# Two transformer blocks on one core: short extra products in TensorE's waits, three condition products moved ahead, and the recurrence's square sums split over two heads

## The chip, the core and the metric

The kernel runs on one core of a Trainium2 chip, in one launch. The metric is the device time of that launch in microseconds (us). The engines named here are TensorE (PE in the profile; its weight loads are PEld), VectorE (DVE), ScalarE (ACT), GpSimd (POOL) and SyncE (SP), which issues the large transfers. TensorE's clock has two levels, 1.2 and 2.4 GHz; the profile shows a granted clock of 0.50 and 1.00 for them.

## The reference

Everything is fp32, for 256 tokens of width 1024. The first block adds three things to x, each computed from a normalised x; the second block takes its result, and a condition vector c:

```
h = _rms(x, mix_norm_g[l])
p = h @ w_in[l]
a_out = _mla(...)                       # 8 heads, latent q and kv
h_out = _hyena(p[..., OFF_HY:], ...)    # long convolutions, here as DFT products
mixed = concatenate([_rms(a_out, ...), _rms(h_out, ...)])
x = x + mixed @ w_out[l]
x = x + _mem_xattn(_rms(x, ...), _rms(mem, ...), ...)   # 4 heads
x = x + _hier_moe(_rms(x, ...), ...)    # 4 groups x 8 experts, top 2 of a group, width 256

mod = silu(c) @ w_ada + b_ada           # six rows of 1024: sh1, sc1, g1, sh2, sc2, g2
u = modulate(x, sh1, sc1)
mix = hybrid_mixer(u, ...)              # gated recurrence (RG-LRU) beside attention of 8 heads
x = layernorm(DEEPNORM_ALPHA * x + g1 * mix, ln1_g, ln1_b)
ffn = hierarchical_moe(modulate(x, sh2, sc2), ...)
x = layernorm(DEEPNORM_ALPHA * x + g2 * ffn, ln2_g, ln2_b)
```

`mod` depends on c alone. The kernel computes it in twelve pieces of 512 columns, the *condition products* `ada(0)` to `ada(11)`, which may stand anywhere ahead of their use.

## The kernel before

**Order of work.** One stream of instructions is written by hand for each engine. TensorE goes, in this order: filter network, latent projection (`lat`), Hyena inputs and filter spectra (`hy0`, `hy1`, `hy2`), latent attention with `ada(0)` to `ada(5)` among its heads, the memory's transposes and projections (`memT`, `mk`, `mv`), output projection `wo`, `ada(6)`, `cT` and `mq`, four heads of cross attention (`xs`, `xT`, `xv`), their projection `mo`, the first mixture of experts, `ada(10)`, `ada(11)`, the inputs of the second block (`xl`, `aq`, `ga`, ...), eight heads of attention with the output projection's pieces (`wpa`, `wpb`) among them, and the second mixture of experts.

**Projections.** A weight arrives in a ring of four slots of SBUF (`ring`), loaded by SP's queue in the order of use. It is split into a high and a low part in fp32r: `high` (L471) on ScalarE, then `low` (L478) on VectorE, in four chunks of 128 x 1024, each holding two row blocks. `three_pass` (L613 to L615) then makes three products of each pair. Chunks 2 and 3 are split into the place of chunks 0 and 1, so ScalarE waits for those to have been used.

**PSUM.** The eight banks are given out by the list `STAGES`: each stage takes the next banks in turn, and `PLACE_AT` holds for each its bank and the number of earlier uses. `take` waits until the bank's earlier user has been read (`bank_free`), `full` and `got` hand it over, `free` gives it back. `transposed` (L598) makes 128x128 transposes by products with the identity `ident`.

**Condition products.** `ada(i)` (L736) is eight products of 32 x 512 in fp32, which the profile shows as 16 records. ScalarE copies the row into the weight's own ring slot (`ada_evac`, L1314), and `ada_col(i)` (L744) makes it a column by four products of one column each (8 records); `modulation(i)` on VectorE (L1851) reads that. The ring slot comes free after `ada_col`.

**A mixture of experts** (`moe(b)`, both times with the same code): transposes `rT` (L598), routing products `rt` (L894, 32 records of 36 columns), the choice of group and experts on VectorE (up to L2100, `hot`), the count of tokens ahead of each (`cnt`, L904 to L908), the selection matrices on VectorE (L2129, L2130, `sel`), the gathering products `gx` (L924), the transposed weights `swT` (L932), and then the loop over the experts: L949 (gate and up), L956, L963 (down) and L969. In the first mixture `ada_col(7)`, `ada(8)` and `ada_col(8)` stand between `rt` and `cnt`, and `ada(9)`, `ada_col(9)` and a bias product (L915) between `cnt` and `gx`.

**Attention of the second block.** Two heads' scores are made ahead (L1117, L1118); then for each head the probabilities are transposed (L1196), the next scores made, some other piece of work done and the values multiplied (L1208, L1209). In head 0 the other piece is `lss`: the sums of squares of the recurrence's output for both halves of the tokens (`token_sums`, L1166), 16 records of one column.

## Time and profile before

| | |
|---|---|
| runs (us) | 1061.04, 1061.32, 1060.31; median 1061.04 |
| profiled execution (us) | 1063.01 |
| its span, first to last instruction (us) | 1061.0 |
| mean granted TensorE clock | 0.955 |
| TensorE busy | 968.9 us (91%) |
| VectorE, ScalarE busy | 584.2 us (55%), 355.7 us (34%) |
| moved by DMA | 289.02 MB, mean 272 GB/s |

The profiled execution took 1.97 us more than the median of the timed runs, and 2.0 us of it lie outside its span. Busy shares are means over stages with different limits. A row of a timeline gives the start of an instruction (or of several alike), its length, its engine, line, kind and operands, and in brackets the idle time of the engine before it with what ended that. Lengths of products overlap, so the step between two starts is the better price of one. A row of windows gives, for a stretch, each engine's busy time, TensorE's granted clock (PEclk) and the DMA's share and rate.

### The profile page before, as it was taken

The numbers are of one execution on the slowest core, as the hardware profiler recorded it, in microseconds if no ns is written. First come the engines' busy times: TensorE is split into PE (matmuls) and PEld (weight loads), VectorE is DVE, ScalarE is ACT, GpSimd is POOL, SyncE is SP. The second block draws the span as 40 slices with busy tenths as digits, with TensorE's granted clock in tenths as the row PEclk, the third lists the DMA queues.
The fourth block names the chain that finished last, engine by engine and source line by source line (L and its number), as shares of the span: only waits on it lengthen the run. The fifth ranks groups of instructions, "written<-read, shape, count | busy, mean of one in ns | idle before, by whom it ended". The sixth has DMA issues, their size and how long they took to land.

```text
span 1061.0 us, 14615 instructions
## 1 busy us (share of the span) xinstructions
PE 968.9 (91%) x5146; PEld 582.0 (55%) x5146; DVE 584.2 (55%) x1104; ACT 355.7 (34%) x684; POOL 20.1 (2%) x41
## 2 busy tenths in 40 slices
PE   6999998999889799999999979898559999999985
PEld 5768556977766433343434569766443343434334
DVE  4735446556345546444444475766774755555545
ACT  5654325346334222222222365743521111111113
POOL 1000001000000000000000000000000000000000
PEclk9999999999997899999999989988769999999998
DMA  9253670455416699999999728530607999999941
GB/s 361 106 237 141 261 308 27 169 201 206 159 54 259 254 364 425 427 423 428 423 427 425 298 80 357 199 120 1 277 1 305 409 427 426 423 427 423 427 175 41
DMA packets 28894, 289.02 MB, mean 272 GB/s; under 512 B 3080, under 2 KB 5544, under 8 KB 7728
## 3 DMA queue, kind: packets, MB, share of 16 engines
q1 hardware_dynamic: 25344, 282.04, 64.9%
q0 software_dynamic: 1136, 3.74, 1.1%
q10 hardware_dynamic: 2368, 2.64, 0.8%
q8 instruction: 28, 0.46, 0.2%
q14 instruction: 18, 0.15, 0.0%
HBM read 287.34 MB, written 1.06 MB: 272 GB/s over the span
## 4 chain that ended last, share of the span: by engine, by line
PE 56%; DVE 6%; ACT 2%; issue 2%; DVEq 0%; ACTq 0%
PE bank L949 22%; PE bank L963 11%; PE bank L969 6%; PE bank L956 4%; PE bank L613 2%; PE bank L614 2%; PE bank L615 2%; PE bank L924 1%; PE bank L1069 1%; DVE ring_r L478 1%; PE bank L1070 1%; PE bank L1024 1%; PE bank L894 0%; PE bank L1208 0%; PE bank L1058 0%
## 5 line engine op out<-in xcount | busy, mean ns | idle before, releaser
L949 PE MATMUL bank<-ring,arena 128*64 128x512 f32 x1040 | 239.2, 602 | 6.6 <-DVE arena L2181 6.6
L478 DVE TENSOR_TENSOR ring_r<-ring,ring_r 128x1024 fp32r<-128x1024 f32 (+1 forms) x84 | 99.2, 1212 | 95.5 <-ACT ring_r L471 95.5
L2195 DVE TENSOR_REDUCE arena<-bank 128x512 f32 x130 | 83.8, 687 | 117.2 <-PE bank L969 114.6
L949 PEld LDWEIGHTS bank<-ring,arena 128*64 128x64 f32 x1040 | 69.8, 137 | 130.4 <-issue 130.4
L963 PE MATMUL bank<-ring,arena 128*64 128x512 f32 x520 | 125.8, 604 | 1.8 <-DVE arena L2317 1.4
L471 ACT ACTIVATE ring_r<-ring 128x1024 fp32r<-128x1024 f32 (+1 forms) x84 | 84.9, 1046 | 84.5 <-PE bank L615 84.0
L613 PE MATMUL bank<-HT_r,ring_r 128*128 128x256 f32 x352 | 103.9, 295 | 9.8 <-DVE arena_r L1795 3.6
L615 PE MATMUL bank<-HT_r,ring_r 128*128 128x256 f32 x352 | 101.9, 290 | 0.0
L1531 ACT ACTIVATE arena<-bank 128x512 f32<-128x512 f32 x64 | 38.3, 598 | 152.5 <-PE bank L949 152.5
L969 PEld LDWEIGHTS bank<-tab,arena 128*128 128x128 f32 x520 | 55.7, 140 | 54.8 <-issue 49.6
L613 PEld LDWEIGHTS bank<-HT_r,ring_r 128*128 128x128 f32 x352 | 70.3, 200 | 12.0 <-issue 10.5
L969 PE MATMUL bank<-tab,arena 128*128 128x128 f32 x520 | 70.9, 279 | 3.3 <-DVE arena L2224 2.1
L1525 ACT ACTIVATE arena<-arena 128x128 f32<-128x128 f32 x64 | 19.8, 309 | 152.7 <-DVE arena L2201 152.7
L615 PEld LDWEIGHTS bank<-HT_r,ring_r 128*128 128x128 f32 x352 | 70.0, 199 | 0.0
L614 PE MATMUL bank<-XN_r,ring_r 128*128 128x256 f32 x224 | 65.2, 291 | 0.0
L963 PEld LDWEIGHTS bank<-ring,arena 128*64 128x64 f32 x520 | 31.7, 136 | 50.8 <-issue 48.3
L956 PEld LDWEIGHTS bank<-tab,arena 128*128 128x128 f32 x260 | 27.2, 141 | 55.0 <-issue 50.3
L2201 DVE TENSOR_REDUCE arena<-bank 128x256 f32<-128x512 f32 x65 | 44.3, 681 | 14.3 <-PE bank L956 14.3
L615 PE MATMUL bank<-ring_r,arena_r 128*128 128x512 f32 x128 | 51.8, 404 | 0.0
L2181 DVE COPY arena<-arena 128x512 f32 x66 | 28.2, 427 | 36.5 <-issue 36.5
L614 PEld LDWEIGHTS bank<-XN_r,ring_r 128*128 128x128 f32 x224 | 45.0, 201 | 0.5 <-issue 0.5
L613 PE MATMUL bank<-ring_r,HT_r 128*128 128x512 f32 (+1 forms) x96 | 39.2, 408 | 5.9 <-DVE ring_r L478 5.1
(424 smaller groups left out, 1370.6 us busy)
## 6 DMA issues: line engine op xcount, KB each, us to landing
ring<-in_experts SPq DMA_DIRECT2D x64, 2048.0 KB, 15.1
ring<-in_experts SPq DMA_DIRECT2D x64, 1024.0 KB, 11.6
ring<-in_ada SPq DMA_DIRECT2D x12, 2048.0 KB, 8.7
ring<-in_win SPq DMA_DIRECT2D x5, 2048.0 KB, 12.8
ring<-in_hy SPq DMA_DIRECT2D x3, 2048.0 KB, 18.7
ring<-in_mk SPq DMA_DIRECT2D x2, 2048.0 KB, 8.5
ring<-in_mv SPq DMA_DIRECT2D x2, 2048.0 KB, 9.6
ring<-in_wo SPq DMA_DIRECT2D x2, 2048.0 KB, 7.4
```

Source lines behind the costliest of these rows:

```text
L471: nc.scalar.activation(R(h), w, ACT.Copy).then_inc(sem("w_high"), 1)
L478: nc.vector.tensor_tensor(R(w), w, R(h), ALU.subtract).then_inc(sem("w_low"), 1)
L613: mm(ps, R(ah), R(bh), start=first, stop=False)
L614: mm(ps, R(ah), R(bl), start=False, stop=False)
L615: return mm(ps, R(al), R(bh), start=False, stop=last_)
L949: last = mm(gu_bank[g:g + WIN, :], xw[:, k, :], w[:, k * 512:(k + 1) * 512], start=k < 2, stop=k >= KD - 2)
L956: last = tr(guT_bank[:, c * P:(c + 1) * P], gu_sb[:, c * P:(c + 1) * P], ident)
L963: last = mm(d_bank[half][64 * f:64 * f + WIN, :], hb[:, f, :], w[:, o:o + 512], start=True, stop=True)
L969: last = tr(dT_bank[c // 4][:, (c % 4) * P:(c % 4 + 1) * P], d_sb[:, c * P:(c + 1) * P], ident)
L1531: A_(gu_sb, gu_bank[:, :], ACT.Copy).then_inc(sem(f"gu_sb{b}"), 1)
L2195: last = V.reduce_sum(ysT[:, 4 * u:4 * u + 4, bass.ds(s, WIN)], dT_bank[u][:, :].rearrange("p (c g w) -> p c w g", c=4, g=2), AXX)
L2201: return V.reduce_sum(three(gu_sum, 4), guT_bank[:, :].rearrange("p (c g w) -> p c w g", c=4, g=2), AXX)
```

## The change

A helper `occupy(stage, j, n)` is added on TensorE. It waits for the bank that stage `stage` will take next, and issues `n` fp32 products of 128x128 by 128x256 into it (16 records for eight of them); the stage's own first product starts anew and overwrites them. It is called in twenty places, for 106 products in all: ahead of the filter network (8), `lat` (5), `hy2` (4), `mk` (5), `cT` (3), `xs0` (2), `xT0` (3), `mo` (1), the first `gx` (6) and the first expert loop (8), `ada(10)` (4), `xl` (4), `aT0` (4), in heads 3 and 4 (4 and 4), `rT2` (21), `cnt2` (8), the second `gx` (8), and the second expert loop (4). The operands are tables that are in SBUF anyway; the first two calls read an area of zeros, `still`, that VectorE sets at its start.

`ada(7)` moves ahead of `mo`, `ada(8)` takes the place of `ada(7)`, `ada_col(7)` goes ahead of the routing products, and `ada_col(8)`, `ada(9)`, `ada_col(9)` all stand between `rt` and `cnt`. ScalarE's copies follow: `ada_evac(7)` before the second half of `mo`'s first weight is split, `ada_evac(8)` where 7 was and `ada_evac(9)` where 8 was. VectorE's `modulation(9)` goes from behind the selection to directly behind the count. The order of SP's loads is unchanged. The list `STAGES` follows, so from `mo` on the stages lie in banks shifted by one.

The sums of squares `lss` are made in two halves, one in head 0 and one in head 1; VectorE's copy of them goes from head 0 to head 1.

```diff
-STAGES += [("mo", 4), ("ada7", 1)]
+STAGES += [("ada7", 1), ("mo", 4), ("ada8", 1)]
...
+            def occupy(stage, j, n, w=ident, x=T("iota")[:, 0:256]):
+
+                b, use = place(stage, j)
+                if use:
+                    pe.wait_ge(sem(f"bank_free{b}"), use)
+                for _ in range(n):
+                    mm(bank[b][:, 0:256], w, x, start=True, stop=True)
...
+            pe.wait_ge(sem("still"), 1)
+            occupy("hT", 0, 8, still[:, 0:P], still[:, P:P + 256])
...
             transposed("hT", XN, KD, "xn_x")
+            occupy("lat", 0, 5, still[:, 0:P], still[:, P:P + 256])
...
+            occupy("hy2", 0, 4)
             channel_out("hy2", ["hy2"], HT, low_x, banks_of("hT"))
...
             transposed("memT", XN, KD, "xn_m")
+            occupy("mk", 0, 5)
...
             ada(6)
+            occupy("cT", 0, 3)
...
+            occupy("xs0", 0, 2)
...
+            occupy("xT0", 0, 3)
...
+            ada(7)
+            occupy("mo", 0, 1)
             token_out("mo", ["mo0", "mo1"], oT, low_m, [(f"xv{h}", 0) for h in range(XH)])
-            ada(7)
+            ada(8)
 
             def moe(b):
+                if b == 2:
+                    occupy("rT2", 0, 21)
                 transposed(f"rT{b}", XN, KD, f"xn_r{b}")
+                if b == 1:
+                    ada_col(7)
...
                 if b == 1:
-                    ada_col(7)
-                    ada(8)
                     ada_col(8)
+                    ada(9)
+                    ada_col(9)
+                else:
+                    occupy("cnt2", 0, 8)
 
                 pe.wait_ge(sem("hot"), b)
...
                 if b == 1:
-                    ada(9)
-                    ada_col(9)
                     pe.wait_ge(sem("onehot"), 32)
...
+                occupy(f"gx{b}", 0, 8 if b == 2 else 6)
...
+                occupy(f"yTa{b}", 0, 8 if b == 1 else 4)
...
+            occupy("xl", 0, 4)
             ada(10)
             ada(11)
             transposed("uT", XN, KD, "xn_u")
+            occupy("xl", 0, 4)
             channel_out("xl", ["win0"], HT, low_x, banks_of("uT"))
...
                     a_scores(1)
+                    occupy("aT0", 0, 4)
...
                 if h == 0:
                     pe.wait_ge(sem("squared"), 4)
-                    full(token_sums(take(pe, "lss"), sq, range(4)), "lss")
+                    lss = take(pe, "lss")
+                    token_sums(lss, sq, range(4), (0,))
+                    wp_ps["lss"] = lss
                 elif h == 1:
+                    full(token_sums(wp_ps["lss"], sq, range(4), (1,)), "lss")
                     pe.wait_ge(sem("lo_low"), 1)
                     wp_lru(0, 0)
                 elif h == 2:
                     wp_lru(0, 1)
+                elif h == 3:
+                    occupy("ap2", 0, 4)
                 elif h in (4, 5):
+                    if h == 4:
+                        occupy("ap2", 0, 4)
                     wp_lru(1, h - 4)
...
             x_out(XH - 1)
+            ada_evac(7)
             high(act, "mo0", (2, 3))
...
-            ada_evac(7)
+            ada_evac(8)
...
                 if b == 1:
-                    ada_evac(8)
+                    ada_evac(9)
                 act.wait_ge(sem("e_diff"), b)
...
+            V.memset(still, 0.0).then_inc(sem("still"), 1)
...
                                      ALU.add), f"cnt{b}")
+                if b == 1:
+                    modulation(9)
...
                 if b == 1:
-                    modulation(9)
                     ready(dve, "adac9")
...
-                if h == 0:
+                if h == 1:
                     ps = got(dve, "lss")
```

Three places on TensorE. The first is the first mixture of experts from the routing products' end (`wr,HT`, 36 columns) to the gathering products (`arena_r`, 512 columns); 32 x 512 is a condition product, 128 x 1 its column, 128 x 32 the count. Before:

```order
L894 MATMUL bank<-wr,HT 128x36
L744 MATMUL bank<-tab,ring 128x1 [waits bank_free6,bank_free0]
L744 MATMUL bank<-tab,ring 128x1 x3
L736 MATMUL bank<-ring,cm 32x512 [waits bank_free7,slot_full0]
L736 MATMUL bank<-ring,cm 32x512 x7
L744 MATMUL bank<-tab,ring 128x1 [waits bank_free0,bank_free7]
L744 MATMUL bank<-tab,ring 128x1 x3
L904 MATMUL bank<-arena,tab 128x32 [waits bank_free1,hot]
...
L736 MATMUL bank<-ring,cm 32x512 [waits bank_free2,slot_full1]
L736 MATMUL bank<-ring,cm 32x512 x7
L744 MATMUL bank<-tab,ring 128x1 [waits bank_free3,bank_free2]
...
L915 MATMUL bank<-HT 8x512 [waits bank_free4,mask_row,onehot]
L924 MATMUL bank<-arena_r 128x512 [waits bank_free5,xn_low,sel1]
```

The same place after the change, where `bank<-tab 128x256` are the added products:

```order
L756 MATMUL bank<-tab,ring 128x1 [waits bank_free0,bank_free1]
L756 MATMUL bank<-tab,ring 128x1 x3
L748 MATMUL bank<-ring,cm 32x512 [waits bank_free1,slot_full1]
L748 MATMUL bank<-ring,cm 32x512 x7
L756 MATMUL bank<-tab,ring 128x1 [waits bank_free2,bank_free1]
L756 MATMUL bank<-tab,ring 128x1 x3
L930 MATMUL bank<-arena,tab 128x32 [waits bank_free3,hot]
...
L939 MATMUL bank<-HT 8x512 [waits bank_free4,mask_row,onehot]
L600 MATMUL bank<-tab 128x256 [waits bank_free5]
L600 MATMUL bank<-tab 128x256 x5
L950 MATMUL bank<-arena_r 128x512 [waits bank_free5,xn_low,sel1]
```

Between `rt` and `cnt` one column, one condition product and one column stand as before, each of the next number; between `cnt` and `gx` a condition product and its column are gone and six added products stand in their place.

The second place is the second mixture of experts after the change, from the last projection to the gathering products. Before, the rows are the same without those of `bank<-tab 128x256`:

```order
L625 MATMUL bank<-ring_r,arena_r 128x512
L600 MATMUL bank<-tab 128x256 [waits bank_free7]
L600 MATMUL bank<-tab 128x256 x20
L608 MATMUL bank<-tab,XN 128x128 [waits bank_free2,bank_free1,normed,bank_free0,bank_free7]
...
L918 MATMUL bank<-wr,HT 128x36
L600 MATMUL bank<-tab 128x256 [waits bank_free4]
L600 MATMUL bank<-tab 128x256 x7
L930 MATMUL bank<-arena,tab 128x32 [waits bank_free4,hot]
...
L600 MATMUL bank<-tab 128x256 [waits bank_free5]
L600 MATMUL bank<-tab 128x256 x7
L950 MATMUL bank<-arena_r 128x512 [waits bank_free5,xn_low,sel2]
```

Each group of added products stands directly ahead of an instruction that waits for another engine.

The third place is heads 0 and 1 of the second block's attention, where 128x1 are the sums of squares. Before, all of them stand in head 0:

```order
L1118 MATMUL bank<-arena 128x256
L1166 MATMUL bank<-tab,arena 128x1 [waits bank_free5,squared]
L1166 MATMUL bank<-tab,arena 128x1 x7
L1208 MATMUL bank<-arena 64x256 [waits bank_free5,bank_free3,bank_free4,bank_free2]
L1209 MATMUL bank<-arena 64x128
L1196 MATMUL bank<-tab,arena 128x128 [waits bank_free2,a_norm]
```

After the change:

```order
L1197 MATMUL bank<-tab,arena 128x1 [waits bank_free5,squared]
L1197 MATMUL bank<-tab,arena 128x1 x3
L1246 MATMUL bank<-arena 64x256 [waits bank_free5,bank_free3,bank_free4,bank_free2]
L1247 MATMUL bank<-arena 64x128
L1234 MATMUL bank<-tab,arena 128x128 [waits bank_free2,a_norm]
L1234 MATMUL bank<-tab,arena 128x128 x2
L1147 MATMUL bank<-arena 128x128 [waits bank_free1]
L1148 MATMUL bank<-arena 128x256
L1197 MATMUL bank<-tab,arena 128x1 x4
L623 MATMUL bank<-ring_r,arena_r 128x512 [waits bank_free7,w_low,bank_free6,lo_low]
```

Half of the one-column products has gone behind head 0's values and head 1's transposes and scores.

## Rows read from the trace of the kernel before

**Rows 1.** The page's part 1: busy time, share of span, instructions.

```profile
PE 968.9 (91%) x5146; PEld 582.0 (55%) x5146; DVE 584.2 (55%) x1104; ACT 355.7 (34%) x684; POOL 20.1 (2%) x41
```

**Rows 2.** Windows: start:end length, busy PE, PEld, DVE, ACT, POOL, PEclk, DMA share, GB/s.

```profile
75.00:85.00 10.00, 7.84 (x55) 7.63 (x54) 6.35 (x11) 7.23 (x13) 0.00 (x0) 0.83 0.84 357
...
296.00:304.00 8.00, 5.00 (x16) 3.83 (x15) 3.56 (x4) 2.38 (x4) 0.00 (x0) 0.79 0.00 0
324.00:370.00 46.00, 39.20 (x188) 24.97 (x188) 25.53 (x74) 13.73 (x32) 1.16 (x3) 0.74 0.70 281
370.00:600.00 230.00, 228.69 (x1164) 92.31 (x1160) 111.47 (x213) 52.26 (x102) 0.00 (x0) 1.00 0.99 416
...
686.00:750.00 64.00, 56.32 (x238) 40.63 (x234) 41.09 (x90) 23.94 (x61) 0.90 (x2) 0.84 0.18 72
750.00:800.00 50.00, 25.60 (x118) 19.73 (x118) 36.34 (x84) 20.50 (x44) 1.12 (x2) 0.73 0.36 145
800.00:1016.00 216.00, 215.64 (x1099) 86.08 (x1100) 122.23 (x231) 29.70 (x64) 0.00 (x0) 1.00 1.00 417
```

**Rows 3.** Waits of PE: line and releaser, us in total, times, longest.

```profile
PE bank L613 <- DVE ring_r L478: 11.2, 5, 3.0
```

**Rows 4.** Timeline of PE, fp32 products of 128x256 at full clock.

```profile
277.51 3.69 PE L864 MATMUL bank<-arena 128*128 128x256 f32 x16 [1.10 <-issue]
```

**Rows 5.** Timeline of PE, the latent projection's first products.

```profile
15.17 0.68 PE L613 MATMUL bank<-ring_r,HT_r 128*128 128x416 f32 x1 [2.77 <-DVE ring_r L478]
...
21.16 0.35 PE L613 MATMUL bank<-ring_r,HT_r 128*128 128x416 f32 x1
21.34 0.35 PE L614 MATMUL bank<-ring_r,HT_r 128*128 128x416 f32 x1
```

**Rows 6.** A window over those products.

```profile
15.00:20.00 5.00, 4.83 (x14) 4.65 (x15) 2.52 (x6) 3.13 (x6) 0.00 (x0) 1.00 0.98 420
```

**Rows 7.** Timeline of PE, the first product of `mo`.

```profile
300.57 0.76 PE L613 MATMUL bank<-ring_r,arena_r 128*128 128x512 f32 x1 [3.00 <-DVE ring_r L478]
```

**Rows 8.** Timeline of PE, first mixture of experts.

```profile
329.45 5.33 PE L894 MATMUL bank<-wr,HT 128*128 128x36 f32 x32 [1.05 <-ACT HT L1259]
...
342.45 0.61 PE L904 MATMUL bank<-arena,tab 128*128 128x32 f32 x2
...
344.70 3.64 PE L736 MATMUL bank<-ring,cm 128*32 128x512 f32 x16
...
351.00 9.18 PE L924 MATMUL bank<-arena_r 128*128 128x512 f32 x32
...
365.33 5.35 PE L949 MATMUL bank<-ring,arena 128*64 128x512 f32 x16 [4.28 <-DVE arena L2181]
```

**Rows 9.** Timeline of DVE, there: second half of the selection.

```profile
348.58 0.75 DVE L2130 SCALAR_TENSOR_TENSOR arena_r<-tab,arena,arena_r 128x512 fp32r<-128x512 f32 x1
```

**Rows 10.** Timeline of PE, the second block's first projection.

```profile
622.16 0.55 PE L613 MATMUL bank<-HT_r,ring_r 128*128 128x256 f32 x1 [2.43 <-DVE XN_r L2382]
```

**Rows 11.** Timeline of PE, attention of the second block.

```profile
688.82 0.47 PE L613 MATMUL bank<-ring_r,HT_r 128*128 128x512 f32 x1 [2.31 <-DVE ring_r L478]
...
697.22 1.95 PE L1166 MATMUL bank<-tab,arena 128*128 128x1 f32 x16
...
716.96 1.11 PE L1208 MATMUL bank<-arena 128*64 128x256 f32 x2 [2.39 <-DVE arena L2509]
...
723.45 0.77 PE L613 MATMUL bank<-ring_r,arena_r 128*128 128x512 f32 x1 [2.54 <-issue]
```

**Rows 12.** Timeline of PE, second mixture of experts.

```profile
761.88 3.35 PE L598 MATMUL bank<-tab,XN 128*128 128x128 f32 x16 [12.31 <-DVE XN L2567]
...
775.03 0.64 PE L904 MATMUL bank<-arena,tab 128*128 128x32 f32 x2 [4.95 <-DVE arena L2100]
...
782.00 9.09 PE L924 MATMUL bank<-arena_r 128*128 128x512 f32 x32 [4.62 <-DVE arena_r L2130]
...
796.01 3.65 PE L949 MATMUL bank<-ring,arena 128*64 128x512 f32 x16 [2.33 <-DVE arena L2181]
```

More of the change, by code:

```diff
@@ L188 @@
     STAGES += [(f"xT{_h}", 1)] + ([(f"xs{_h + 2}", 1)] if _h + 2 < XH else []) + [(f"xv{_h}", 1)]
-STAGES += [("mo", 4), ("ada7", 1)]
+STAGES += [("ada7", 1), ("mo", 4), ("ada8", 1)]
 def _moe_stages(b):
-    ada = [[(f"ada{i}", 1), (f"adac{i}", 1)] if b == 1 else [] for i in (8, 9)]
-    return [(f"rT{b}", 4), (f"rt{b}", 1)] + [("adac7", 1)] * (b == 1) + ada[0] + [(f"cnt{b}", 1)] + ada[1] + [("bias", 1)] * (b == 1) + [(f"gx{b}", 8), (f"swT{b}", 2)] \
+    one = b == 1
+    return [(f"rT{b}", 4)] + [("adac7", 1)] * one + [(f"rt{b}", 1)] + [("adac8", 1), ("ada9", 1), ("adac9", 1)] * one \
+        + [(f"cnt{b}", 1)] + [("bias", 1)] * one + [(f"gx{b}", 8), (f"swT{b}", 2)] \
         + [("g2r", 2)] * (b == 2) + [(f"yTa{b}", 4), (f"sct{b}", 4), (f"yTb{b}", 4)]
@@ L336, in two_blocks @@
         prod = three(area(13312, 1024), TT)
+        still = area(12288, 384)
         krb = three(area(13312, 256), TT)
@@ L936, in moe @@
                     gate_row("g2r", diag2, "diag2")
+                occupy(f"yTa{b}", 0, 8 if b == 1 else 4)
+                if b == 2:
                     for j in range(2):
@@ L1160, in wp_attention, with token_sums @@
                     full(last, *stage)
-            def token_sums(ps, src, chunks):
-                for t in range(TT):
+            def token_sums(ps, src, chunks, ts=range(TT)):
+                for t in ts:
                     for i in chunks:
@@ L1498, in moe @@
                 if b == 1:
-                    ada_evac(9)
                     ps = got(act, "bias")
```

## The prediction

> **What bounds the kernel now.** I read the busy times first: TensorE works 91% of the span, the others 55% or less [rows 1], so TensorE's stream sets the time, and only two things can shorten it: fewer or shorter waits, and products that run at the higher clock. The table of windows comes next [rows 2]. In both expert loops TensorE is busy for 228.69 of 230 us and 215.64 of 216 at granted clock 1.00. These 446 us can't gain; they move with their start. The clock is below 1.00 elsewhere. It has two levels, so a mean of 0.84 over 64 us means 64 x (1 - 0.84) / 0.5 = 20.5 us at 1.2 GHz. In the same way the six shorter windows hold: 3.4 us (75:85), 3.4 (296:304), 23.9 (324:370), 20.5 (686:750), 27.0 (750:800); 170:180 and 600:630 look like the first (0.83, 0.89). Whoever works through such a stretch at 2.4 GHz saves half of its busy part. Third come the timelines around them. Nearly all of these stretches begin with a wait of TensorE of 2.2 to 12.3 us for VectorE or ScalarE: 2.77 [rows 5], 3.00 [rows 7], 4.28 [rows 8], 2.43 [rows 10], 2.31, 2.39 and 2.54 [rows 11], 12.31, 4.95 and 4.62 [rows 12]. Five waits for the split of a weight alone are 11.2 us [rows 3]. The exception is the loop's second start: 2.33 us idle, and yet its first 16 records take 3.65 us, where those of the first loop took 5.35 after 4.28 [rows 8, 12]. So an idle time above some 2 us costs the clock in most cases, not in all.
>
> **Price of a product added.** Sixteen records of 128x256 in fp32, which are eight products, take 3.69 us at the higher clock [rows 4]: 0.44 us a product with the tail of the last, and so 0.88 at 1.2 GHz. Where a wait is longer than its products the cost is nothing, since TensorE would stand still. VectorE's memset at the start is cover too: TensorE waits for a DMA there.
>
> **Part by part, as gains in us.**
> Start. `lat` begins cold after 2.77 us: 14 records in 4.83 us are 0.345 each, against 0.18 later [rows 5, 6]. Fifteen such steps at the higher clock would give 2.4. Five products in front take 2.2 us warm and 4.4 cold, 1.6 more than the wait, so the bounds are +2.4 and -1.6; I take 0.5, because the products in front are themselves the cold ones.
> The Trainium skill, "TensorE: Matmul & The Clock Gate", Part 1, warns that the clock recorded in trn2 traces can be unreliable. The row of the window agrees: it shows 1.00 where the steps are twice as long. By the record alone this term would be nothing, by the steps it is up to 2.4.
> `hy2` and `mk`. Each has some 3.4 us at 1.2 GHz (75:85, and 170:180 like it [rows 2]) behind a wait; the one of `hy2` is among the five for a split weight, 2.2 us in the mean and 3.0 the longest [rows 3]. Half of 3.4 is 1.7, the bound. The other bound is the overrun, 4 x 0.88 - 2.2 = 1.3 and 5 x 0.88 - 3.0 = 1.4 lost. The waits are short against what a cold start takes, so not all is saved: 1.3 and 1.2.
> `cT`, `xs0`, `xT0`: two or three products in front of waits of 1 to 2 us, no cold stretch behind: 0 (+0.3 to -0.8 together).
> `mo`. The moved `ada(7)`, 16 records of 32x512, lies now in the wait of 3.00 [rows 7] with one product more: at half of the cold price of the same form (3.64, [rows 8]) 1.9 + 0.4 = 2.3, it fits. ScalarE's copy of it falls where ScalarE has nothing to do until chunk 0 is used. Window 296:304 gives 1.7 at most, and chunk 2's split follows chunk 0's end, so the gain passes on: 1.6; worst -1.0 (4.0 cold against 3.0).
> First routing. Between `rt` and `cnt` the same number of columns and condition products stands as before, so with the clock as it is `cnt` starts as before. What changes is behind it. The selection was done at 348.58 + 0.75 = 349.33, but TensorE came to `gx` only at 351.00, since `ada(9)` began at 344.70 [rows 8, 9]: 1.7 us late. With `ada(9)` gone, the six products and the bias fill 4.6 us; cold at first, they are done near 349.7. That gives 1.3. `gx` took 9.18 with half of it cold, about 7.3 if warm: 1.9 more, if the six products raise the clock. Against it VectorE's `modulation(9)` now stands in front of the selection (0.2). If the clock even holds through `rt`, the way from 329.45 to `cnt` (13.0) loses up to 4 more; VectorE's choice then is the limit. Bounds 0 and 7.0. The 36-column products let the clock fall in both mixtures, so I take near the low end: 2.5.
> First expert. Eight products, 3.5 us warm, fit in 4.28; 5.35 becomes 3.65 [rows 8, 12]: 1.7. The loop's loads start when the columns of the condition products are made, which is earlier as well, so the loop doesn't run into them, though its DMA share is 0.99.
> `xl`. Behind 2.43 us [rows 10] the cold stretch is 6.6 us (600:630 at 0.89), but its second half waits for a weight chunk that ScalarE splits after other work. Bounds +1.5 and -1.0: 0.
> Attention. The 20.5 cold us of window 686:750 are three stretches, by the steps of the single products: 3.4 behind 688.82, 6.6 from 700, the rest from 717. Products in front of 688.82 save 1.5; the sixteen one-column records at 697.22 stand right ahead of the second stretch (half is 3.3), and halving them may or may not keep the clock; the weight's split follows the scores by 5.6 us and takes back 0.8 of it. The products in front of 716.96 change nothing by themselves, as 723.45 waits for VectorE's chain; those in front of that save 1.7 [rows 11]. Bounds 3.2 - 1.3 of overruns = 1.9, and 5.7: 4.0.
> Second routing. 21 products last 9.2 us, of 12.31 idle. 3.1 us stay idle, so the transposes (3.35) probably start cold as before: 0, at best 1.3. Eight products in 4.95: half cold, as `rt` ends cold, 4 x 0.88 + 4 x 0.44 = 5.3, 0.3 over; `cnt` warm saves 1.1. Eight in 4.62, warm, fit; `gx` from 9.09 to some 7.3: 1.8. Sum 2.6, less a part for a clock that may not rise in time: 2.2; bounds -2.1 (eight cold products, 7.0) and 3.9. Four products in 2.33 fit, and the loop was warm already: 0.
> The skill's same page, Part 4, says of TensorE's transpose mode that it doesn't count as busy for the clock. The row shows them once only, at 3.35 us behind a long idle time [rows 12], which fits both. If the 16 transposes behind the 21 products were idle in that sense, the products would have been for nothing and `rt` would start cold: the second routing would then give 1.3 instead of 2.2.
>
> Sum: 0.5 + 1.3 + 1.2 + 1.6 + 2.5 + 1.7 + 4.0 + 2.2 = 15.0. The profiled 1063.01 becomes 1048.0; it lies 1.97 over the median, so the timed runs go from 1061.04 to 1046.0.
>
> **The rivals.**
> *Half is given back.* The clock still falls behind short waits, and ScalarE's and VectorE's chains take over in attention and routing, whose ends don't depend on TensorE's clock. For it: L478 releases five waits, and 716.96 and 723.45 are of that kind. Against: the first expert and both `gx` need only the clock. Half of 15: 1053.5.
> *All waits keep the clock.* Upper bounds but for the start: 1.0 + 1.6 + 1.6 + 1.7 + 6.0 + 1.7 + 1.0 + 5.5 + 3.5 = 23.6, 1037.4. For it: almost every cold stretch stands behind a wait that is now filled. Against: the narrow products of 36, 32 and 1 columns remain.
> *Slower: the added products run at 1.2 GHz.* They stand behind narrow or short work, at 0.88 each. Overruns: `lat` 1.6, `hy2` 1.3, `mk` 1.4, `mo` 1.0, first `gx` 1.7, first expert 7.0 - 4.3 = 2.7, `xl` 1.1, `aT0` 1.2, heads 1.1 and 1.0, `cnt2` 2.1, second `gx` 2.4, second loop 1.2, together 19.8. In place of that, what follows would be warm at half of these places at least, since the products went before it, about 8: 1061 + 12 = 1073. It decides from a step of over 0.6 us a product at most places. Against: 0.23 to 0.44 in every wide fp32 stretch that follows warm work, as most waits do.
> *Nothing happens.* The clock follows something other than the waits, and the waits swallow all products: 1061. Only the later `gx` against `ada(9)` speaks for a gain even then, 1.3, so this is nearly excluded.
>
> **How the numbers follow.** Forecast 0.55; half given back 0.22; all waits warm 0.15; slower 0.06; nothing 0.02. Range 1038 to 1055. It holds the forecast, most of the half and the greater part of the full gain. A measurement of this kernel can tell about 0.2%, 2.1 us, from no change: faster by more 0.92, within it 0.03, slower 0.05.
>
> **What would show it.** Right: a granted clock of 1.00 in the stretches behind `hy2`, `mk` and `mo`; 0.44 us a product in the groups of `mo`, the first expert and the second `gx`; the first 16 records of the first loop in 3.65; `gx` starting within 0.5 us of the selection, and both in under 8 us; 324:370 shortened by over 4. Wrong: products of 0.88 that end after their wait; the clock at 0.50 in 717:727 or behind 689 as before; a loop that waits for its weights. If the gain is under 8, the terms of attention and of first routing are those to doubt.

## The result, and the profile after

The changed kernel took 1053.12 us (median of 11 runs, 1048.18 to 1058.38), the kernel before 1061.67 us beside it (11 runs). The ratio is 0.990, 95% interval 0.9872 to 0.9929: 7.5 to 13.6 us faster, where 15.0 were forecast, 1046.0 with a range of 1038 to 1055. The medians are 8.6 us apart, the two profiled spans 9.8. (The text on the change says that the added products stand in twenty places; its list has nineteen.)

TensorE's row of busy times after the change (before: [rows 1]). Its busy time grows by 35.0 us. The 212 added records alone take 56.3 us, so the rest of its work got 21 us shorter.

```profile
PE 1003.9 (96%) x5358; PEld 611.3 (58%) x5358; DVE 584.0 (56%) x1105; ACT 355.2 (34%) x684; POOL 20.2 (2%) x41
```

The same windows as in [rows 2], in the same columns (start:end length, busy PE, PEld, DVE, ACT, POOL, granted clock, DMA share, GB/s):

```profile
75.00:85.00 10.00, 9.57 (x72) 8.94 (x71) 7.54 (x12) 7.21 (x13) 0.00 (x0) 1.00 0.70 295
...
296.00:304.00 8.00, 7.48 (x33) 5.99 (x33) 3.40 (x4) 2.86 (x4) 0.00 (x0) 1.00 0.00 1
324.00:370.00 46.00, 43.77 (x194) 29.39 (x196) 23.63 (x71) 11.52 (x25) 1.17 (x3) 0.78 0.71 293
370.00:600.00 230.00, 228.36 (x1167) 95.72 (x1164) 113.91 (x216) 52.50 (x102) 0.00 (x0) 1.00 0.98 411
...
686.00:750.00 64.00, 60.45 (x265) 44.97 (x264) 40.26 (x84) 24.12 (x60) 0.90 (x2) 0.89 0.24 92
750.00:800.00 50.00, 44.16 (x215) 29.98 (x213) 33.65 (x84) 17.19 (x36) 1.12 (x2) 0.93 0.40 153
800.00:1016.00 216.00, 214.31 (x1094) 86.38 (x1092) 124.55 (x234) 27.23 (x60) 0.00 (x0) 1.00 0.97 409
```

The windows around `hy2` and `mo` went from 0.83 and 0.79 to 1.00. The stretch of the first routing hardly moved, 0.74 to 0.78, and attention little, 0.84 to 0.89. Those two are where the forecast was too high.

The sharpest view is the start of the instruction at the same place in both traces. Each difference is the sum of all gains before it:

| instruction | before | after | difference |
|---|---|---|---|
| filter network's second layer, behind the first part of `lat` | 22.38 | 20.99 | -1.39 |
| `mk`, first product | 174.90 | 172.19 | -2.71 |
| `mo`, first product | 300.57 | 296.66 | -3.91 |
| condition product behind `mo` (`ada(7)` before, `ada(8)` after) | 324.33 | 318.83 | -5.50 |
| first `gx` | 351.00 | 346.09 | -4.91 |
| first `swT` | 360.01 | 353.58 | -6.43 |
| `ada(10)`, behind the first mixture | 613.08 | 604.95 | -8.13 |
| columns of `ada(10)`, behind `xl` | 636.41 | 629.11 | -7.30 |
| first `av` product | 688.82 | 681.49 | -7.33 |
| square sums, head 0 | 697.22 | 689.09 | -8.13 |
| `wp0`, first product, head 1 | 702.30 | 695.05 | -7.25 |
| last projection's piece behind head 4 | 723.45 | 716.81 | -6.64 |
| transposes of the second mixture | 761.88 | 755.00 | -6.88 |
| second `gx` | 782.00 | 773.36 | -8.64 |
| second loop, first product | 796.01 | 785.84 | -10.17 |
| span | 1061.0 | 1051.2 | -9.8 |

TensorE's timeline after the change, at the places of [rows 7, 8]:

```profile
296.66 0.47 PE L623 MATMUL bank<-ring_r,arena_r 128*128 128x512 f32 x1 [0.52 <-DVE ring_r L480]
...
323.95 5.64 PE L918 MATMUL bank<-wr,HT 128*128 128x36 f32 x32 [0.26 <-ACT HT L1297]
...
337.26 0.61 PE L930 MATMUL bank<-arena,tab 128*128 128x32 f32 x2
...
341.31 5.13 PE L600 MATMUL bank<-tab 128*128 128x256 f32 x12
346.09 7.65 PE L950 MATMUL bank<-arena_r 128*128 128x512 f32 x32
...
358.90 3.65 PE L977 MATMUL bank<-ring,arena 128*64 128x512 f32 x16 [0.83 <-DVE arena L2221]
```

`mo` waits 0.52 us instead of 3.00, and its first product takes 0.47 instead of 0.76. The first expert's records take 3.65 instead of 5.35. The six products ahead of `gx` took 5.13 us, 0.80 each by the step from their start to that of `gx`: the granted clock is 0.50 from 341.3 to 345.3 and rises in the last of them (0.68 in 345.3 to 346.3). VectorE was done long before they ended:

```profile
334.26 0.23 DVE L2139 TENSOR_TENSOR arena<-arena 128x64 f32<-128x64 f32 x1
...
343.39 0.75 DVE L2171 SCALAR_TENSOR_TENSOR arena_r<-tab,arena,arena_r 128x512 fp32r<-128x512 f32 x1
```

The choice (`hot`) was there at 334.5 and the count started at 337.26, 2.8 us late; the selection was there at 344.1 and `gx` started at 346.09, 2.0 late.

`xl`, where the second chunk ends, the third begins, and the clock falls [rows 10]:

```profile
619.74 0.28 PE L625 MATMUL bank<-HT_r,ring_r 128*128 128x256 f32 x1
621.79 0.36 PE L623 MATMUL bank<-HT_r,ring_r 128*128 128x256 f32 x1 [1.77 <-DVE ring_r L480]
...
622.48 0.41 PE L625 MATMUL bank<-HT_r,ring_r 128*128 128x256 f32 x1
```

Attention [rows 11]:

```profile
679.11 1.99 PE L600 MATMUL bank<-tab 128*128 128x256 f32 x8
681.49 0.47 PE L623 MATMUL bank<-ring_r,HT_r 128*128 128x512 f32 x1 [0.39 <-DVE ring_r L480]
...
689.09 1.02 PE L1197 MATMUL bank<-tab,arena 128*128 128x1 f32 x8 [0.73 <-ACT arena L1345]
...
690.92 0.90 PE L1234 MATMUL bank<-tab,arena 128*128 128x128 f32 x3
...
693.33 1.86 PE L1197 MATMUL bank<-tab,arena 128*128 128x1 f32 x8
695.05 0.77 PE L623 MATMUL bank<-ring_r,arena_r 128*128 128x512 f32 x1
...
700.45 0.86 PE L1246 MATMUL bank<-arena 128*64 128x256 f32 x2
...
716.81 0.47 PE L623 MATMUL bank<-ring_r,arena_r 128*128 128x512 f32 x1 [2.37 <-issue]
717.12 0.40 PE L624 MATMUL bank<-ring_r,arena_r 128*128 128x512 f32 x1
...
718.07 0.63 PE L625 MATMUL bank<-ring_r,arena_r 128*128 128x512 f32 x1
```

The stretch behind 681.49 is warm now, but 0.73 us of that are waited off at once: TensorE comes to the square sums before ScalarE's squares are ready, a wait that did not exist. By 690.92 the clock is down (0.90 against 0.55 for these three transposes at full clock), so the second half of the square sums costs 1.86 us where one half costs 1.02 warm. Behind 716.81 the clock falls after five products.

The eleven runs of the changed kernel say the same in another way. Their spans go from 1046.2 us at a granted clock of 0.981 to 1056.2 at 0.968; a straight line through all eleven has 0.80 us per 0.001 of clock and a correlation of -0.99. What differs from run to run is mainly how long the clock is low. A single trace, and the table above, are one draw of that. At most places they are good for some 1 us; at the first routing and in `xl` for less, as the traces of the experiments show at their end.

### The profile page after: what moved, and what is told of

Same layout as the page of the kernel before. It is cut to its first block, busy times and chain, and to the rows that moved or that the text cites. A ratio compares the mean times of both kernels' runs of the same rounds, so it can differ in the third digit from the quotient of the medians.

```text
span 1051.2 us, 15040 instructions
## 1 busy us (share of the span) xinstructions
PE 1003.9 (96%) x5358; PEld 611.3 (58%) x5358; DVE 584.0 (56%) x1105; ACT 355.2 (34%) x684; POOL 20.2 (2%) x41
## 4 chain that ended last, share of the span: by engine, by line
PE 54%; DVE 7%; ACT 2%; issue 2%; DVEq 0%; ACTq 0%
PE bank L977 22%; PE bank L991 11%; PE bank L997 6%; PE bank L984 4%; PE bank L623 2%; PE bank L625 2%; PE bank L624 2%; DVE ring_r L480 1%; PE bank L950 1%; PE bank L1097 1%; PE bank L1098 1%; PE bank L1052 1%; PE bank L1246 0%; PE bank L1197 0%; PE bank L918 0%
## 5 line engine op out<-in xcount | busy, mean ns | idle before, releaser
L623 PE MATMUL bank<-HT_r,ring_r 128*128 128x256 f32 x352 | 101.9, 290 | 6.0 <-DVE ring_r L480 3.1
L625 PE MATMUL bank<-HT_r,ring_r 128*128 128x256 f32 x352 | 100.3, 285 | 0.0
L997 PE MATMUL bank<-tab,arena 128*128 128x128 f32 x520 | 70.9, 279 | 3.3 <-DVE arena L2264 2.1
L623 PEld LDWEIGHTS bank<-HT_r,ring_r 128*128 128x128 f32 x352 | 68.2, 194 | 8.9 <-issue 7.3
L625 PEld LDWEIGHTS bank<-HT_r,ring_r 128*128 128x128 f32 x352 | 68.2, 194 | 0.0
L600 PE MATMUL bank<-tab 128*128 128x256 f32 x186 | 47.7, 409 | 0.0
L984 PE MATMUL bank<-tab,arena 128*128 128x128 f32 x260 | 42.6, 286 | 2.1 <-ACT arena L1569 1.4
```

The costliest lines, as they stand in the source:

```text
L600: mm(bank[b][:, 0:256], w, x, start=True, stop=True)
L623: mm(ps, R(ah), R(bh), start=first, stop=False)
L625: return mm(ps, R(al), R(bh), start=False, stop=last_)
L984: last = tr(guT_bank[:, c * P:(c + 1) * P], gu_sb[:, c * P:(c + 1) * P], ident)
L997: last = tr(dT_bank[c // 4][:, (c % 4) * P:(c % 4 + 1) * P], d_sb[:, c * P:(c + 1) * P], ident)
```

## The experiments

Theory A is the prediction's: the added products keep the clock for what follows. Rival B: the moved condition products carry the gain. All experiments are compared with the kernel before on the same chip.

**e1_moves_only.** Moves and split stay, the products go.

```diff
             def occupy(stage, j, n, w=ident, x=T("iota")[:, 0:256]):
-                b, use = place(stage, j)
...
+                return
```

> The changed kernel without any of the 106 added products; the moved condition products and the split square sums stay. Theory A (the gain is TensorE's clock behind filled waits): only ada(7) in the wait ahead of mo (up to 1.6 us) and the routing without ada(9) ahead of gx (up to 1.5) are left, so about 1058 to 1061 against 1061.0 before, and the first expert's 16 records are at 5.3 us again. Rival B (the moved condition products carry the gain): 1053 to 1055.

Measured: 1061.26 us against 1061.39, ratio 0.9997 (0.9975 to 1.0018). The moved parts together are worth nothing that can be measured. That is a sum of two: from `mo`'s first product to the condition product behind it this trace takes 22.17 us, as the changed kernel does, where the kernel before took 23.76, so `ada(7)` alone fills that wait and is worth 1.6 us; the split of the square sums takes about as much back (e3_lss_whole). The first expert is cold again behind its old wait:

```profile
360.09 5.35 PE L973 MATMUL bank<-ring,arena 128*64 128x512 f32 x16 [4.29 <-DVE arena L2217]
```

**e2_fill_only.** The kernel before with the products alone.

```diff
+            occupy("mo", 0, 5)
             token_out("mo", ["mo0", "mo1"], oT, low_m, [(f"xv{h}", 0) for h in range(XH)])
...
+                if b == 2:
+                    occupy("gx2", 0, 8)
```

> The kernel before with the added products alone, at the same places and in the same numbers, but 5 ahead of mo (ada(7) isn't there to fill that wait) and none ahead of the first gx, where TensorE comes late anyway. Theory A: start 1.4, hy2 and mk 2.5, mo 1.6, first expert 1.7, second routing 2.4, attention and xl near 0: about 9.5 off, 1051.5 (1050 to 1054). Rival B: under 3 off, 1058 or more.

Measured: 1051.04, ratio 0.9921 (0.9892 to 0.9951). The whole gain, or as much as can be told, comes with the products. Rival B falls; what the moved `ada(7)` wins at `mo`, five products win there as well (22.19 us).

**e3_lss_whole.** The square sums in head 0 again.

```diff
-                    lss = take(pe, "lss")
-                    token_sums(lss, sq, range(4), (0,))
-                    wp_ps["lss"] = lss
+                    full(token_sums(take(pe, "lss"), sq, range(4)), "lss")
```

> The changed kernel with the sixteen one-column square sums all in head 0 again. Theory C (splitting them doesn't hold the clock, as it fell in head 0 all the same, and the second half then costs 1.86 us at 1.2 GHz): the same as the changed kernel or up to 1 us faster. Rival D (the split is worth something, my term of the prediction): slower by 1.5 to 3 us.

Measured: 1051.61, ratio 0.9909 (0.9883 to 0.9935), against 0.990 for the changed kernel. The times can't decide, since the 1.5 to 3 us of rival D lie within the interval. The traces can. From the first square sum to the values of head 1 it takes 10.02 us here:

```profile
688.02 1.92 PE L1197 MATMUL bank<-tab,arena 128*128 128x1 f32 x16 [0.72 <-ACT arena L1342]
...
698.04 0.65 PE L1243 MATMUL bank<-arena 128*64 128x256 f32 x2
```

With the split it takes 11.36 us (689.09 to 700.45). The other traces agree: whole sums 10.01 to 10.08 (before, e2, e3, e6, e7, e8), split ones 11.36 to 11.64 (after, e1, e5, e10, e11). The exception is e9, where the clock held through both halves (6.93). The 1.5 us are still there at the second mixture's transposes, 64.34 us behind the first sum here and 65.91 in the changed kernel. Rival D falls: the split is a loss of some 1.5 us, more than theory C had.

**e4_narrow.** Two products of one column for each of 256.

```diff
-                for _ in range(n):
-                    mm(bank[b][:, 0:256], w, x, start=True, stop=True)
+                for _ in range(2 * n):
+                    mm(bank[b][:, 0:1], w, x[:, 0:1], start=True, stop=True)
```

> The changed kernel with each added product of 256 columns replaced by two of one column each, which take TensorE about as long (8 records of one column took 0.95 us before, so 0.48 for two products against 0.44). Theory E (the clock looks at how much is computed, not at whether TensorE is idle): the waits are filled but the clock falls as before, so most of the gain of the filling is lost: 1058 to 1061, first expert 5.3 us. Rival F (any instruction in the wait keeps the clock): 1053 as the changed kernel.

Measured: 1071.30, ratio 1.0098 (1.0066 to 1.0131), worse than either expected. The expectation took their warm price. At 1.2 GHz two such products last 0.9 us, and the 42 ahead of the transposes last longer than the wait of 12.3 there: 15.8 us, and not 19 as the next expectation says.

```profile
747.40 15.84 PE L600 MATMUL bank<-tab 128*128 128x1 f32 x84
763.10 3.65 PE L608 MATMUL bank<-tab,XN 128*128 128x128 f32 x16
```

No time is idle ahead of these transposes, and they are as slow as behind 12.31 us of idle time. The cleanest place is the first expert:

```profile
356.61 3.63 PE L600 MATMUL bank<-tab 128*128 128x1 f32 x32
361.06 5.07 PE L977 MATMUL bank<-ring,arena 128*64 128x512 f32 x16 [0.82 <-DVE arena L2221]
```

The narrow products last as long as the wide ones (3.63 against 3.62) and leave as much idle (0.82 against 0.83), at a granted clock of 1.00 until 360, and yet the expert's records take 5.07 against 3.65. So theory E holds in the traces; the time mixes it with the overruns, so it was run again with one for one.

**e10_narrow_once.** The same, `range(n)`.

> The changed kernel with each added product narrowed from 256 columns to one, one for one; such a product takes 0.24 us warm and 0.46 cold, so nothing overruns its wait, unlike in e4_narrow, where two for one at 1.2 GHz took 19 us in a wait of 12. Theory E (the clock falls although TensorE isn't idle): as e1_moves_only, 1059 to 1062. Rival F (filling the wait with anything is enough): 1053 to 1055.

Measured: 1062.96, ratio 1.0008 (0.9985 to 1.0031): nothing is left of the gain. TensorE's timeline, first mixture:

```profile
344.56 2.72 PE L600 MATMUL bank<-tab 128*128 128x1 f32 x12
347.44 10.13 PE L950 MATMUL bank<-arena_r 128*128 128x512 f32 x32 [0.17 <-DVE arena_r L2171]
...
358.29 1.84 PE L600 MATMUL bank<-tab 128*128 128x1 f32 x16
...
362.74 5.35 PE L977 MATMUL bank<-ring,arena 128*64 128x512 f32 x16 [2.61 <-DVE arena L2221]
```

`gx` takes 10.13 against 7.65 behind products of 256 columns. The clock was already at 0.50 when the six began, in both kernels; the wide ones brought it up just ahead of `gx`, the narrow ones did not, and `gx` is as slow as in e1 with nothing there (10.35). At other places the shorter products leave much idle, 2.61 us ahead of the first expert and 7.73 ahead of the second mixture's transposes, so there this run can't tell narrow work from idle time; e4's traces can. The time fits theory E: nothing is left of the gain when the products have one column.

**e5_routing.** Work that isn't awaited leaves the way to the count.

```diff
                     ada_col(8)
-                    ada(9)
-                    ada_col(9)
...
+                    ada(9)
+                    ada_col(8)
...
                 if b == 1:
+                    ada_col(9)
                     pe.wait_ge(sem("onehot"), 32)
...
-                occupy(f"gx{b}", 0, 8 if b == 2 else 6)
+                occupy(f"gx{b}", 0, 8 if b == 2 else 1)
```

> The changed kernel with the first routing in another order: between rt and the count stand ada(9) and then ada_col(8) (5.5 us cold, for a choice on VectorE of 4.9), behind the count ada_col(9), the bias product and 1 added product instead of 6; modulation(9) back behind the selection. Theory G (in the changed kernel TensorE comes 2.9 us late to the count and 2.0 late to gx, for work that could stand elsewhere): the count starts within 0.6 us of the choice, gx within 0.5 of the selection, some 4 us earlier; gx itself stays at 1.2 GHz longer, +1.5; net 2 to 3 us faster than the changed kernel, 1050. Rival H (gx's start doesn't matter, the clock takes it all back): as the changed kernel, 1053.

Measured: 1047.42, ratio 0.9868 (0.984 to 0.9896). TensorE's timeline:

```profile
328.16 3.46 PE L748 MATMUL bank<-ring,cm 128*32 128x512 f32 x16
331.55 1.05 PE L756 MATMUL bank<-tab,ring 128*128 128x1 f32 x8
333.19 0.41 PE L929 MATMUL bank<-arena,tab 128*128 128x32 f32 x2 [0.58 <-DVE arena L2139]
...
339.34 8.61 PE L950 MATMUL bank<-arena_r 128*128 128x512 f32 x32 [0.34 <-DVE arena_r L2169]
```

From the routing products' end to `gx` it is now 11.2 us (328.16 to 339.34), where the changed kernel took 16.7 (329.40 to 346.09); `gx` itself gives 1.0 back. TensorE now waits for VectorE at both places, as it should. Theory G holds in the trace. The gain over the changed kernel is 3.4 us by the ratios, whose intervals overlap.

**e6_att_rT2_empty.** e2 without the products in attention (heads 3 and 4 too, not shown) and without the 21.

```diff
-                    occupy("aT0", 0, 4)
...
-                if b == 2:
-                    occupy("rT2", 0, 21)
```

> The kernel before with the added products alone (as in e2_fill_only), but without those in attention (ahead of aT0, in heads 3 and 4) and without the 21 ahead of rT2. Theory I (attention is bounded by VectorE's and ScalarE's chain and by the cold stretch behind the one-column products, which the fillers don't reach; rT2's products end 3 us before the transposes): no slower than e2_fill_only by more than 1 to 1.5 us, 1052. Rival J (my term of 4 us for attention holds and other noise hid it): 1055 or more.

Measured: 1054.12, ratio 0.9932 (0.9911 to 0.9952) against 0.9921 for e2: 1.2 us, inside the interval. In time these 33 products can't be told from nothing. The traces say more. From the first square sum to the second mixture's transposes e2 takes 64.38 us and e6 65.71; the kernel before, without them as well, took 64.66. So the products of heads 3 and 4 win between 0.3 and 1.3. At the second `gx` the two are level again (768.74 and 768.81), since in e2 the eight products ahead of the count ran at 1.2 GHz (6.37 us) and ended 1.1 us after VectorE's choice (761.82, the count at 762.92). The transposes with the 21 products, and without:

```profile
736.37 9.23 PE L599 MATMUL bank<-tab 128*128 128x256 f32 x42
748.84 3.42 PE L607 MATMUL bank<-tab,XN 128*128 128x128 f32 x16 [3.24 <-DVE XN L2601]
```

```profile
750.10 3.65 PE L607 MATMUL bank<-tab,XN 128*128 128x128 f32 x16 [12.31 <-DVE XN L2594]
753.73 3.96 PE L912 MATMUL bank<-wr,HT 128*128 128x36 f32 x32
```

With 3.24 us left idle the transposes are nearly as slow as behind 12.31.

**e7_more_fill.** e2 with the remaining waits filled (also 10 products instead of 8 ahead of the second `gx`, not shown).

```diff
+            channel_out("xl", ["win0"], HT, low_x, banks_of("uT"),
+                        between=lambda c: occupy("adac10", 0, 4) if c == 1 else None)
...
-                        occupy("ap2", 0, 4)
+                        occupy("ap2", 0, 8)
...
-                    occupy("rT2", 0, 21)
+                    occupy("rT2", 0, 28)
```

> As e2_fill_only with more added products: 4 between the second and third chunk of xl (a wait of 1.8 us that is new, in which the clock falls), 8 instead of 4 in head 4 (2.4 us left), 28 instead of 21 ahead of rT2 (3.2 us left), 10 instead of 8 ahead of the second gx (1.3 left). By theory A each keeps the clock for what follows: xl 1.7, head 4 1.6, transposes and rt 1.5 to 2, gx 0.2: 5 us off e2_fill_only, 1046 to 1047. Rival K (these stretches are bounded by the chains of ScalarE and VectorE, a warm TensorE only waits longer): 1051.

Measured: 1048.83, ratio 0.9876 (0.9849 to 0.9902), 4.8 us under e2 by the ratios, 2.2 by the medians, the intervals overlapping. The transposes:

```profile
736.32 12.25 PE L599 MATMUL bank<-tab 128*128 128x256 f32 x56
748.79 1.94 PE L607 MATMUL bank<-tab,XN 128*128 128x128 f32 x16 [0.22 <-DVE XN L2603]
751.33 5.29 PE L915 MATMUL bank<-wr,HT 128*128 128x36 f32 x32 [0.61 <-ACT HT L1296]
```

They are warm, 1.94 for 3.42, but 0.61 is waited off and the 36-column products lose the clock in their midst (5.29 for 4.44): of 1.5 us, 1.2 remain at the count. In head 4, with eight products and 0.64 us idle, the twelve products of the weight take 2.93 us instead of 4.51 and the 1.5 us gained reach the transposes (62.83 us behind the first square sum, 64.38 in e2). At `xl` nothing was won: from its first product to the columns of conditions it takes 13.54 us here and 13.57 in e2, where the clock had held behind 1.75 us of idle time. Theory A holds where the stretch was cold, and the sizes are smaller than thought.

**e11_gx1_none.** The changed kernel without the six products ahead of the first `gx` (`8 if b == 2 else 0`).

> The changed kernel without the six products ahead of the first gx, which ran at 1.2 GHz there (5.1 us) and ended 2 us after the selection. Theory L (an added product that delays real work costs its whole time, the same work cold costs half): gx starts 2 us earlier and has 2 to 3 us more at 1.2 GHz: 0.5 to 1 us faster than the changed kernel, 1052.5. Rival M (they warm gx and pay for themselves): 1 us slower, 1054.

Measured: 1050.95, ratio 0.9894 (0.9858 to 0.993), the changed kernel's 0.990.

```profile
343.14 10.09 PE L950 MATMUL bank<-arena_r 128*128 128x512 f32 x32 [2.86 <-issue]
```

`gx` starts 2.95 us earlier and takes 2.44 longer. This trace was ahead by 0.95 us at the condition product behind `mo` (317.88 against 318.83) and is ahead by 0.51 at `swT` (353.07 against 353.58), so here the six products are worth 0.4 us, less than one pair of traces can tell. Neither theory L's gain nor M's loss is shown; the six products about pay for themselves.

**e9_double.** Twice as many products everywhere (`range(2 * n)`).

> The changed kernel with twice as many added products everywhere. What my slower rival rested on, measured by itself: products beyond a wait cost TensorE 0.44 us each if the clock is up, 0.88 if not. 106 more are 46.6 us at 0.44; about 14 us of idle time are left at these places to take them, and stretches that were still cold (xl, head 4, the transposes of rT2) become warm, about 4: 1053 + 47 - 14 - 4 = 1082 (1078 to 1086) if the clock stays up. 1110 or more if the products themselves run at 1.2 GHz.

Measured: 1065.69, ratio 1.0026 (0.9995 to 1.0057), 16 us less than expected. The price per product was right: the added records take 101.4 us of TensorE against 56.3, so 0.43 us for each of the 106 more. What was wrong is that an overrun travels on to the end. Against the changed kernel the trace is 10.8 us late at the first expert and 9.8 at the square sums, but only 4.4 at the values of head 5 (725.57 against 721.19). Of these 5.4 us, 4.4 are won up to the values of head 1, where the clock held, and the rest in waits for VectorE and ScalarE that got shorter. By the second expert loop it is 13.7 us late, for the products ahead of the second mixture's transposes, count and `gx` overrun their waits too. In all, 45 us of added work cost 13.6 us of span. The prediction's rival that had the change slower at 1073 summed its overruns in the same way, so it was probably priced too high as well.

**e8_all.** The changed kernel with the square sums whole, e5's order and e7's additions.

> The changed kernel with the square sums whole, e5's routing and e7's additions: if both hold, 1053 - 2.5 - 5 = 1045 to 1046; if neither, 1052.

Measured: 1046.03, ratio 0.9847 (0.9818 to 0.9876), the lowest: 16 us under the kernel before, 5.6 us under the changed one by the ratios. Its interval overlaps those of e5 and e7. Its profiled span is 1042.8 us at a granted clock of 0.984.

**What the traces say together.** Each line is a stretch of TensorE's stream, from the start of one instruction to the start of another, by trace:

| stretch | us |
|---|---|
| first mixture, `rt` to `swT`, order of the kernel before | before 30.56, e7 27.83, e2 27.74, e6 26.14 |
| the same, order of the changed kernel | after 29.63, e3 29.62; without wide products e11 30.06, e10 30.04, e1 28.45 |
| the same, order of e5 | e5 25.01, e8 24.96 |
| `xl`, first product to the columns of conditions | before 14.25; after and e11 15.08, e3 15.06; e1, e2, e5 13.57, e6, e8 13.56, e7 13.54, e10 13.53 |
| first square sum to the second mixture's transposes, sums whole | before 64.66, e6 65.71, e2 64.38, e3 64.34, e7 62.83, e8 62.82 |
| the same, sums split | after 65.91, e11 66.00, e5 66.02, e10 66.37, e1 66.42 |
| first expert, its first 16 records | 3.65 in the eight with wide products ahead; before, e1, e10 5.35; e4 5.07 |

The same instructions in the first routing took from 26.14 to 30.56 us, and the trace of the kernel before is the longest of the four. `xl` took 13.5 or 15.1 us in the changed kernel's variants, with products in its waits or without. So a single pair of traces settles neither place.

## Why the prediction was right, and where it was not

Direction and mechanism were right: the gain comes with the added products (e1, e2), and it goes when they have one column (e4, e10). The size was about two thirds, and the measured time lies near the upper end of the range. Of the terms, with what the table of starts shows for each:

Start, 0.5 taken: 1.4. `lat` began 0.9 us later but warm. Here the steps between products, 0.19 us instead of 0.345, told the truth, and not the record of the clock, which is 1.00 in both.

`hy2` and `mk`, 1.3 and 1.2: 1.3 and 1.2. `mo`, 1.6: 1.6. First expert, 1.7: 1.7. The reading was: a window's mean clock gives the cold time, half of its busy part is the gain, if the wait in front takes the products. It held wherever the work behind the wait was wide and TensorE alone bounded it.

First routing, 2.5: 0.9. The step that failed is "cold at first, they are done near 349.7": the six products ran at 1.2 GHz to nearly their end, behind work that had been at 1.2 GHz since the routing products, and `gx` came 2.0 us after the selection. I had seen that the 36-column products let the clock fall, and didn't carry it on to the six. Also not seen: the columns of conditions behind `rt` made the count 2.8 us late, before and after; e5 took those. Even the 0.9 is against the slowest of four traces of the old order; against the other three (26.1 to 27.8 us) the changed order, at 29.6, is slower.

`xl`, 0: -0.8. In this trace the clock fell in a new wait of 1.77. In e2 it held behind 1.75, so this loss is a draw of the single trace.

Attention, 4.0: -0.45. This is the mis-sized term, the largest of the sum and 4.4 of the 5 us missing. The saving of 1.5 behind 688.82 was there, and half of it was waited off at ScalarE's squares (0.73). "Halving them may or may not keep the clock": it did not. The clock fell 1.6 us behind the first square sum (690.7, at 0.84 in 690 to 691), 2.7 us behind it before, the second half was then made at half speed, and the split lost 1.5 us (e3). And "those in front of that save 1.7": four products left 2.37 us idle and the clock fell five products on; with eight instead of four, e7 gained 1.5 of these 1.7. As they stand, the products in heads 3 and 4 are worth 0.3 to 1.3 us by the traces (e6), and nothing that the times can tell.

Second routing, 2.2: 3.3, for the most part by `cnt` and `gx` warm, as reasoned: 0.9 from the count to `gx` and 1.5 from `gx` to the loop. The rest is 0.5 at the transposes and 0.3 up to the count; whether that comes of the 21 products isn't shown.

Of the signs that were named, these came: a clock of 1.00 behind `hy2`, `mk` and `mo`, some 0.45 us a product ahead of the first expert and of the second `gx`, the first loop's 3.65, both `gx` under 8 us. These did not: the first `gx` started 2.0 us after the selection, and from the condition product behind `mo` to the first expert it is 40.07 us instead of 41.00, nothing near 4 less.

Of the rivals, "half is given back" at 1053.5 came nearest in time; by the ratio, 10.6 us, the gain lies about midway between it and the forecast. Its reason is there in part: 0.73 us are waited off at ScalarE's squares. What it lacks is that clock was lost behind narrow work too, in the first routing and in head 0. That its figure comes so near is in part luck, since the loss at `xl` is a draw. The slower case did not come, because its products were warm at most places. In the kernel before, TensorE did nothing from 749.6 to 761.88 and then nothing but the 16 transposes until 765.2, and the granted clock rose among them (0.50 until 764, 0.61 in 764 to 765, 1.00 behind); in e7 they ran warm throughout behind 28 products. So these traces don't bear out for these transposes what the Trainium skill, "TensorE: Matmul & The Clock Gate", Part 4, says of the transpose mode, that it doesn't count as busy for the clock.

## What to carry to other kernels

Where an engine's clock depends on its work, look for waits ahead of wide work and fill them to the end with wide throwaway products; here a group that left 3 us idle was worth almost nothing, and one with one column nothing. Fill only waits that are there: first move work that nobody awaits out of the way of what VectorE awaits (3.4 us here by the ratios), then fill what remains. Count a gain only up to the next instruction that waits for another engine's chain, and check that the work behind isn't narrow. Before one place is judged by one pair of traces, compare the same stretch in several.

## What the runs showed of the hardware

Work of one column in TensorE's waits lost the higher clock as if little had run: behind 32 records of one column and 0.82 us of idle time the first expert took 5.07 us, behind 16 of 256 columns, as long in time, and 0.83 us of idle time 3.65 (e4). The clock fell in the midst of the 36-column products of the first mixture too, with 0.26 us of idle time ahead of them (granted clock 1.00 in 324 to 325, 0.73 in 325 to 326, 0.50 behind). Narrow work doesn't always cost it: in e9, with no idle time ahead, twice eight records of one column took 1.05 us each and the clock stayed at 1.00.

Idle times of 1.31 us (second `gx`) and 1.75 (`xl` in e2) kept the clock, 1.77 (`xl` in the changed kernel) and 2.37 (head 4) lost it a few products on, and 2.33 ahead of the second loop kept it in the kernel before.

The granted clock varies between runs of one program, 0.968 to 0.981 here, and 0.80 us of span go with each 0.001. With such a spread, five rounds settle some 3 us, and not the single places; those only the traces tell, and several of them.

That the first `gx` costs about the same with six cold throwaway products in front of it as without them (e11) was unexpected: the products cost 2.0 us of start, and `gx`, which without them has a granted clock of 0.50 for its first 5 us, gives them back.
